# Two head transposes ahead of the fourth mLSTM numerator, and w_out's first tile begun with its pool rows in both banks

## The chip, the cores and the metric

The kernel runs on one core of one Trainium2 chip. The metric is the device time of one execution in microseconds, the median of several runs of the same program; lower is better. A core has a matrix engine (TensorE, PE in the profile; its weight loads are PEld), a vector engine (VectorE, DVE), a scalar engine (ScalarE, ACT), GpSimd (POOL) and SyncE (SP), which here issues most of the DMAs. Each works through its own queue in order; semaphores tie the queues together.

## What is computed

One inference step of a two-layer decoder for 512 prompt tokens and 8 sample tokens, all in float32. The first layer mixes by two parallel groups of channels, a causal pooling mixer and an mLSTM with four heads; both halves of the mix go through one output projection w_out (1024 x 1024). After it comes a mixture-of-experts layer with 32 experts, two per token; then an S5 state space layer with a GLU, a second mixture of experts and a last norm. Cut to the part that matters here:

```python
pool_out, pb = _pool_mixer(z[..., :o1], ...)            # 512 channels, four groups of 128
ml_out, c1, n1, m1 = _mlstm_mixer(...)                  # 512 channels, four heads of 128
mix = jnp.concatenate([pool_out, ml_out], axis=-1).astype(x.dtype) @ w['w_out_ab'][e]
x = x + mix.astype(x.dtype)
x = x + _hmoe(_rmsnorm(x, w['norm_ffn'][l]), ...)

# in _pool_mixer
y = jnp.einsum('btgc,gcd->btgd', d, pool_w.astype(jnp.float32)).reshape(uf.shape)
return y * pool_scale.astype(jnp.float32), ext[:, -POOL_BUF:]

# in _mlstm_chunk, for one chunk of 128 tokens
num = jnp.einsum('bhls,bhsd->bhld', s, v) + w_inter[..., None] * jnp.einsum('bhvk,bhlk->bhlv', c, q)
h = num / jnp.maximum(jnp.abs(den), jnp.exp(-m_row))[..., None]
# at the end of _mlstm_mixer
return hs * jax.nn.sigmoid(o_pre.astype(f32)), c1, n1, m1
```

## The kernel before, in words

The 512 prompt tokens are four chunks of 128. In the stage that the change touches, each chunk c gives a numerator product `num c` (TensorE, L797 and L799, with the denominators as a 129th column), which VectorE divides and stores as rows of heads, HM (L1754 to L1760, the body of one loop over c). TensorE then transposes the four heads of the chunk (`hT c`, in the helper `transposes`, L705), and VectorE multiplies them by the output gate into MIX (L1770, a second loop over c). MIX has eight blocks of 128 rows: blocks 0 to 3 are the pooling half, blocks 4 to 7 the heads. The pooling half comes from four products `pw g` (TensorE, L810), which ScalarE scales into MIX with three instructions each (L1353, L1355, L1357).

All of these results pass through a ring of four PSUM slots of two banks each. `jobs_of_kernel` lists the jobs in the order in which they take slots, with the engine that empties each; a job waits until the job four places ahead of it in that list has been emptied. So the order of the list, which has to be the order of TensorE's program, decides who waits for whose slot. Behind the last `hT`, the router stage gets the same four slots under fixed roles; ROLES names the jobs that were last in them.

The router stage computes `main(k)` for five tiles of tokens: MIX times w_out, 16 matmuls of 128x512 in four quarters of four (L863; each f32 matmul leaves two records in the trace, a transpose one). `main(0)` and the first quarter of `main(1)` come first, then the transposes of tile 0 (L880), which read X and so wait until VectorE has added tile 0's product to it (L1845, the function `mixed`). Router logits are L893, position matmuls L904 and L906, the gathering of the first experts' rows L934. The router of layer 1 uses the same code.

On VectorE, behind the four L1770, come a memset (L1849), three products of 128x4096 (at L1605, the line of the helper `tt`) for the state of the sample tokens, which need two broadcasts from DRAM (scratch_sdk, scratch_sdd), and then the router: `produce(0)` is `mixed(0)`. SyncE loads w_out when `z 19` is full, the broadcasts when `pw 3` is full, and four small S5 loads when `num 3` is full; GpSimd waits for the last of these with its S5 preparation (L2246). The experts' weights are asked for when the last tile has been mixed.

## Time and profile before

| what | us |
|---|---|
| median of 3 runs | 1092.79 |
| lowest run | 1092.39 |
| highest run | 2146.93 |
| the profiled execution, its own time | 1091.85 |
| its span | 1090.0 |
| TensorE busy in the span | 950.8 (87%) |
| VectorE busy | 416.2 (38%) |
| ScalarE busy | 182.8 (17%) |
| GpSimd busy | 375.8 (34%) |

The span runs from the first to the last instruction of one profiled execution; all times in rows are counted from its start. Busy times of TensorE are of pipelined matmuls with modelled ends, so they overlap. The stage in question lies between 190 and 305 us. A row that gives an idle time in square brackets names what ended it.

### The profile page before, as it was taken

How to read it: one execution, taken by the hardware profiler on the slowest of the kernel's cores; microseconds unless marked ns; L12 is line 12 of the kernel's file. 1: busy time of each engine (PE TensorE's matmuls, PEld its weight loads, DVE VectorE, ACT ScalarE, POOL GpSimd, SP SyncE). 2: the span in 40 equal slices, each digit the busy share in tenths (PEclk: the TensorE clock that was granted, in tenths of full speed). 3: DMA queues.
4: the chain of work that ended last, by engine and by line, in shares of the span. 5: the costliest groups of instructions: out<-in, count | busy, mean ns of one | idle time of the engine just before them, and what ended most of it. 6: DMA issues, size and time to landing. Idle time of an engine off the chain costs nothing.

```text
span 1090.0 us, 15860 instructions
## 1 busy us (share of the span) xinstructions
PE 950.8 (87%) x5716; PEld 577.3 (53%) x5716; DVE 416.2 (38%) x913; ACT 182.8 (17%) x353; POOL 375.8 (34%) x647
## 2 busy tenths in 40 slices
PE   3999989899897888787788499999989999787786
PEld 3788879545554444444444466444455555344342
DVE  5301155757752222232227762123465223221217
ACT  5311021222210000000016421102351000000003
POOL 1278900283256666656551730000020221101000
PEclk9999999899898999999999789999979999999998
DMA  7126860650669999999994744703047999999965
GB/s 257 39 78 218 295 259 3 254 183 20 247 265 395 423 420 416 421 402 409 393 364 145 110 107 182 328 29 146 19 182 275 421 421 424 423 424 425 425 270 214
DMA packets 45920, 292.39 MB, mean 268 GB/s; under 512 B 10609, under 2 KB 12017, under 8 KB 26391
## 3 DMA queue, kind: packets, MB, share of 16 engines
q1 hardware_dynamic: 35463, 270.29, 62.8%
q0 software_dynamic: 8640, 16.03, 3.9%
q10 hardware_dynamic: 1760, 5.31, 1.5%
q8 instruction: 35, 0.57, 0.2%
q14 instruction: 22, 0.18, 0.0%
HBM read 270.47 MB, written 36.80 MB: 282 GB/s over the span
## 4 chain that ended last, share of the span: by engine, by line
PE 56%; DMA 28%; DVE 6%; SPq 4%; issue 3%; POOL 2%; ACT 1%; POOLq 0%; DVEq 0%; ACTq 0%
DMA arena<-in_w_gu 18%; PE ps L739 13%; PE ps L863 10%; PE ps L1007 9%; PE ps L1204 5%; DMA arena<-in_w_down 4%; PE ps L997 3%; SPq L570 2%; DMA arena<-scratch_hd,idx_now 2%; PE ps L934 2%; PE ps L1162 2%; PE ps L1158 2%; DMA arena<-scratch_kp 2%; PE ps L893 2%; POOL arena L2345 2%
## 5 line engine op out<-in xcount | busy, mean ns | idle before, releaser
L1007 PE MATMUL ps<-arena 128*64 128x256 f32 x2048 | 239.1, 389 | 52.8 <-DMA arena<-in_w_gu 52.6
L1007 PEld LDWEIGHTS ps<-arena 128*64 128x64 f32 x2048 | 148.5, 140 | 143.9 <-DMA arena<-in_w_gu 44.7
L2246 POOL TENSOR_TENSOR arena<-arena 128x32 f32<-128x32 f32 (+5 forms) x232 | 117.5, 506 | 171.3 <-DMA arena<-in_s_d 73.8
L2345 POOL TENSOR_TENSOR arena<-arena 128x256 f32<-128x256 f32 (+3 forms) x192 | 132.7, 691 | 41.7 <-POOL arena L2345 41.4
L739 PE MATMUL ps<-arena 128*128 128x260 f32 x640 | 141.7, 383 | 0.0
L997 PE MATMUL ps<-arena 128*64 128x512 f32 x512 | 124.7, 631 | 13.8 <-DMA arena<-in_w_down 13.2
L739 PEld LDWEIGHTS ps<-arena 128*128 128x128 f32 x640 | 121.1, 190 | 18.7 <-issue 0.4
L863 PE MATMUL ps<-arena 128*128 128x512 f32 x256 | 118.7, 616 | 3.9 <-DVE arena L1770 3.7
L1989 DVE TENSOR_TENSOR arena<-arena,ps 128x128 f32<-128x128 f32 x64 | 18.3, 288 | 256.2 <-ACT arena L1454 256.1
L1454 ACT ACTIVATE arena<-ps 128x128 f32<-128x128 f32 x64 | 17.8, 278 | 467.8 <-PE ps L1007 467.8
L863 PEld LDWEIGHTS ps<-arena 128*128 128x128 f32 x256 | 48.6, 196 | 61.2 <-issue 60.1
L997 PEld LDWEIGHTS ps<-arena 128*64 128x64 f32 x512 | 37.6, 144 | 79.3 <-issue 68.2
L1605 DVE TENSOR_TENSOR arena<-arena 128x32 f32<-128x32 f32 (+17 forms) x101 | 62.4, 617 | 35.1 <-DMA arena<-scratch_rows 21.9
L2011 DVE TENSOR_TENSOR arena<-ps,arena 128x512 f32<-128x512 f32 x60 | 41.5, 691 | 77.2 <-PE ps L997 77.2
L428 POOL TENSOR_TENSOR arena<-arena 128x4 f32<-128x4 f32 (+1 forms) x8 | 1.6, 201 | 190.8 <-DVE arena L2218 164.4
L2388 POOL COPY idx_now<-idx_dest 128x1 int32 (+1 forms) x30 | 5.5, 184 | 167.0 <-DVE arena L2011 167.0
L1204 PE MATMUL ps<-arena 128*128 128x512 f32 x128 | 55.4, 593 | 0.4 <-DVE arena L2188 0.4
L958 PE MATMUL ps<-arena 128*128 128x128 f32 x256 | 38.7, 276 | 6.2 <-DMA arena<-scratch_hd,idx_now 6.1
L705 PE MATMUL ps<-arena 128*128 128x128 f32 (+6 forms) x218 | 26.9, 275 | 18.4 <-DVE arena L1244 15.2
L2379 POOL DMA_INDIRECT arena<-scratch_hd,idx_now x30 | 32.2, 1074 | 26.0 <-POOL idx_now L2376 26.0
L1927 DVE TENSOR_TENSOR arena<-ps,arena 128x512 f32<-128x512 f32 x64 | 41.0, 681 | 0.3
L1204 PEld LDWEIGHTS ps<-arena 128*128 128x128 f32 x128 | 24.2, 190 | 30.2 <-issue 29.4
(225 smaller groups left out, 975.1 us busy)
## 6 DMA issues: line engine op xcount, KB each, us to landing
arena<-in_w_gu SPq DMA_DIRECT2D x64, 2048.0 KB, 13.2
arena<-in_w_down SPq DMA_DIRECT2D x64, 1024.0 KB, 14.0
arena<-in_w_in SPq DMA_DIRECT2D x10, 1024.0 KB, 5.9
scratch_yd<-arena SPq DMA_DIRECT2D x2, 4160.0 KB, 18.6
arena<-scratch_yd SPq DMA_DIRECT2D x16, 512.0 KB, 7.3
arena<-in_w_out SPq DMA_DIRECT2D x1, 4096.0 KB, 12.2
scratch_hd<-arena ACTq DMA_DIRECT2D x8, 512.0 KB
arena<-in_w_glu SPq DMA_DIRECT2D x2, 2048.0 KB, 7.7
```

The lines of the kernel that those rows point to most:

```text
L739: mm = pe.matmul(o[:, b, 0:HALF], w[:, kc, (n % 2) * P:(n % 2 + 1) * P], HT[:, kc, b * HALF:(b + 1) * HALF], start=kc == 0, stop=kc == KC - 1)
L863: mm = pe.matmul(o[:, b, :], tokens_of(kc, i), w[:, kc, b * 512:(b + 1) * 512], start=kc == 0, stop=kc == KC - 1)
L958: mm = pe.transpose(ps[:, b, q * P:(q + 1) * P], XG[l][half][:, kc * P:(kc + 1) * P], ident)
L997: mm = pe.matmul(ps[CAP * s:CAP * s + CAP, 6 + b, :], AT[l][s][:, CAP * f:CAP * f + CAP], WD[l][i][b][:, 2 * s + f], start=f == 0, stop=f ...
L1007: mm = pe.matmul(ps[CAP * f:CAP * f + CAP, 2 + s, 0:256], XT[l][:, kc, CAP * s:CAP * s + CAP], WGU[l][i][s][:, kc, 256 * f:256 * f + 256], ...
L1204: mm = pe.matmul(o[0:n, b, :], YT[:, kc, i * P:i * P + n], WGL[0][:, kc, b * 512:(b + 1) * 512], start=kc == 0, stop=kc == KC - 1)
L1605: step(v.tensor_tensor(out, a, b, op))
L1927: v.tensor_tensor(XT[l][:, 4 * b:4 * b + 4], ps[:, b, :].rearrange("p (k t) -> p k t", k=4), spread(GK[:, l, 4 * b:4 * b + 4], P), ALU.mul ...
L2011: v.tensor_tensor(YE[l][half][:, 512 * b:512 * b + 512], ps[:, 6 + b, :], w, ALU.mult).then_inc(sem(f"y_ready_{l}"), 1)
L2246: step(g_.tensor_tensor(out, a, b, op))
L2345: g_.tensor_tensor(o, x, y, f).then_inc(sem("matrix_steps"), 1)
L2379: g_.indirect_dma_start(out=XG[l][half], out_offset=None, in_=hd, in_offset=bass.IndirectOffsetOnAxis(ap=now, axis=0), bounds_check=NT - 1 ...
```

## The change

Three things change, all in the order of work.

In the list of jobs and in TensorE's program, `hT 0` comes behind `pw 1`, `hT 1` behind `pw 2`, and `hT 2` behind `num 3`. `hT 3` is issued inside `main(0)`, behind its first quarter. ROLES names the new last four jobs of the ring.

The quarters of the first tile (k == 0, in both layers' routers) go through the banks in turn: contraction blocks 0 to 3 for bank 0, then for bank 1, then blocks 4 to 7 for bank 0, then for bank 1. Before, a bank was completed ahead of the other. The waits are spread over the quarters: the first for the pool rows, the third for `hT 3` to have been written out.

On VectorE, the first loop handles chunks 0 to 2, then heads 0 and 1 are written out, then chunk 3 is divided, then heads 2 and 3 are written out.

```diff
-    j += [(("pw", g), "act") for g in range(4)]
-    j += [(("num", 3), "dve")]
-    j += [(("hT", c), "dve") for c in range(TILES)]
+    j += [(("pw", 0), "act"), (("pw", 1), "act"), (("hT", 0), "dve"), (("pw", 2), "act"), (("hT", 1), "dve")]
+    j += [(("pw", 3), "act"), (("num", 3), "dve"), (("hT", 2), "dve"), (("hT", 3), "dve")]
...
-            jobs = [("hT", c) for c in range(TILES)] if l == 0 else [("gl", 0, i) for i in range(1, 5)]
+            jobs = [("pw", 3), ("num", 3), ("hT", 2), ("hT", 3)] if l == 0 else [("gl", 0, i) for i in range(1, 5)]
...
-            for g in range(4):
+
+            def pool_product(g):
                 pe.wait_ge(sem("pool_mixed"), g + 1)
                 ring.wait_free(pe, "pw", g)
...
-            numerator(3)
-            for c in range(TILES):
+
+            def heads(c):
                 ring.wait_emptied(pe, "num", c)
-                ring.wait_free(pe, "hT", c)
                 o = slot("hT", c)
                 transposes(("hT", c), [(o[:, 0, h * P:(h + 1) * P], HM[:, c, h]) for h in range(H)])
+            pool_product(0)
+            pool_product(1)
+            heads(0)
+            pool_product(2)
+            heads(1)
+            pool_product(3)
+            numerator(3)
+            heads(2)
             pe.wait_ge(sem("w_out_in"), 16)
-            for g in range(4):
-                ring.wait_emptied(pe, "pw", g)
-            ring.wait_emptied(pe, "hT", TILES - 1)
...
-                        b, k0 = q // 2, 4 * (q % 2)
+                        b, k0 = (q // 2, 4 * (q % 2)) if k else (q % 2, 4 * (q // 2))
...
-            router(0, MIX, lambda kc, i: MIX[:, kc, i * P:(i + 1) * P], WOUT, lambda q: None)
+            def mixed_ready(q):
+                if q == 0:
+                    for g in range(4):
+                        ring.wait_emptied(pe, "pw", g)
+                elif q == 1:
+                    heads(3)
+                elif q == 2:
+                    ring.wait_emptied(pe, "hT", TILES - 1)
+            router(0, MIX, lambda kc, i: MIX[:, kc, i * P:(i + 1) * P], WOUT, mixed_ready)
...
-            ring.wait_emptied(dve, "z", 19)
-            for c in range(TILES):
+
+            def heads_out(c):
                 take(dve, "hT", c)
...
+            for c in range(3):
+                heads_of(c)
+            ring.wait_emptied(dve, "z", 19)
+            heads_out(0)
+            heads_out(1)
+            heads_of(3)
+            heads_out(2)
+            heads_out(3)
```

TensorE, from the first pool product to the first w_out matmuls, with the semaphores that a row waits for (psum_emptied_by_dve and psum_emptied_by_act are the slots given back by VectorE and by ScalarE). Before, the end of the stage, from the last numerator's last product on (L705 are the head transposes, of which the first three groups read alike and one stands; L863 is w_out):

```order
L799 MATMUL ps<-arena 128x129
L705 MATMUL ps<-arena 128x128 [waits psum_emptied_by_act,psum_emptied_by_dve]
L705 MATMUL ps<-arena 128x128 x3
...
L705 MATMUL ps<-arena 128x128 [waits psum_emptied_by_dve]
L705 MATMUL ps<-arena 128x128 x3
L863 MATMUL ps<-arena 128x512 [waits psum_emptied_by_act,psum_emptied_by_dve,w_out_in]
L863 MATMUL ps<-arena 128x512 x15
```

The same place after the change, from the numerator's last product on (head transposes are now L704, w_out L867):

```order
L798 MATMUL ps<-arena 128x129
L704 MATMUL ps<-arena 128x128 [waits psum_emptied_by_act,psum_emptied_by_dve]
L704 MATMUL ps<-arena 128x128 x3
L867 MATMUL ps<-arena 128x512 [waits psum_emptied_by_act,w_out_in]
L867 MATMUL ps<-arena 128x512 x3
L704 MATMUL ps<-arena 128x128 [waits psum_emptied_by_dve]
L704 MATMUL ps<-arena 128x128 x3
L867 MATMUL ps<-arena 128x512 x4
L867 MATMUL ps<-arena 128x512 [waits psum_emptied_by_dve]
L867 MATMUL ps<-arena 128x512 x7
```

Two groups of head transposes have gone from here to places between the pool products, the fourth group stands behind the first quarter of w_out, and the wait for VectorE is in front of the third quarter. Ahead of the numerator, TensorE after the change, from the second pool product (L810) to the fourth:

```order
L810 MATMUL ps<-arena 128x260 [waits psum_emptied_by_act,pool_mixed]
L810 MATMUL ps<-arena 128x260
L704 MATMUL ps<-arena 128x128 [waits psum_emptied_by_dve]
L704 MATMUL ps<-arena 128x128 x3
L810 MATMUL ps<-arena 128x260 [waits psum_emptied_by_dve,pool_mixed]
L810 MATMUL ps<-arena 128x260
L704 MATMUL ps<-arena 128x128 [waits psum_emptied_by_act,psum_emptied_by_dve]
L704 MATMUL ps<-arena 128x128 x3
L810 MATMUL ps<-arena 128x260 [waits psum_emptied_by_act,pool_mixed]
L810 MATMUL ps<-arena 128x260
```

Before, the four pool products stood here one behind the other, and the numerator behind them. On VectorE, before, from the scaling of the fourth numerator (L1760) to the addition of tile 0 (L1845):

```order
L1760 TENSOR_SCALAR arena<-ps,arena 128x128 [waits dve_steps] x4
L1770 TENSOR_TENSOR arena<-ps,arena 128x4x32x4 [waits psum_full,psum_emptied_by_act,psum_emptied_by_dve]
L1770 TENSOR_TENSOR arena<-ps,arena 128x4x32x4 [waits psum_full,psum_emptied_by_dve] x3
L1849 MEMSET arena 128x1744 [waits psum_emptied_by_dve]
L1605 TENSOR_TENSOR arena<-arena 128x4096 [waits c0_in,kb_in,dve_steps]
L1605 TENSOR_TENSOR arena<-arena 128x4096 [waits dve_steps] x2
L1845 TENSOR_TENSOR arena<-arena,ps 128x1024 [waits dve_steps,routed]
```

After, from the scaling of the third numerator (now L1773) to the same addition (L1866):

```order
L1773 TENSOR_SCALAR arena<-ps,arena 128x128 [waits dve_steps] x4
L1783 TENSOR_TENSOR arena<-ps,arena 128x4x32x4 [waits psum_full,psum_emptied_by_act,psum_emptied_by_dve]
L1783 TENSOR_TENSOR arena<-ps,arena 128x4x32x4 [waits psum_full,psum_emptied_by_dve]
...
L1773 TENSOR_SCALAR arena<-ps,arena 128x128 [waits dve_steps] x4
L1783 TENSOR_TENSOR arena<-ps,arena 128x4x32x4 [waits psum_full,psum_emptied_by_dve] x2
L1870 MEMSET arena 128x1744 [waits psum_emptied_by_dve]
L1617 TENSOR_TENSOR arena<-arena 128x4096 [waits c0_in,kb_in,dve_steps]
L1617 TENSOR_TENSOR arena<-arena 128x4096 [waits dve_steps] x2
L1866 TENSOR_TENSOR arena<-arena,ps 128x1024 [waits dve_steps,routed]
```

Two of the four output products stand ahead of the fourth numerator's steps; the memset, the three long products and the addition follow as they did.

## Rows read from the trace of the kernel before

**Rows 1.** The page: span, and shares of the chain that ended last.
```profile
span 1090.0 us, 15860 instructions
...
PE 56%; DMA 28%; DVE 6%; SPq 4%; issue 3%; POOL 2%; ACT 1%; POOLq 0%; DVEq 0%; ACTq 0%
```
**Rows 2.** Chain of waits, 180 to 300 us: start us, us, what.
```profile
208.90 20.02 PE ps L863 x40
...
229.79 3.44 PE ps L863 x8
```
**Rows 3.** Timeline of TensorE, 182 to 330: start, us, engine, line, tiles, count, idle before.
```profile
195.75 2.79 PE L810 MATMUL ps<-arena 128*128 128x260 f32 x12
199.06 1.11 PE L810 MATMUL ps<-arena 128*128 128x260 f32 x4 [0.51 <-DVE arena L1760]
...
201.80 1.16 PE L705 MATMUL ps<-arena 128*128 128x128 f32 x8
...
208.90 20.02 PE L863 MATMUL ps<-arena 128*128 128x512 f32 x40 [3.73 <-DVE arena L1770]
228.75 1.04 PE L880 MATMUL ps<-arena 128*128 128x128 f32 x8
...
292.57 10.96 PE L934 MATMUL ps<-arena 128*128 128x512 f32 x20
```
**Rows 4.** Timeline of VectorE, 186 to 320 us.
```profile
195.05 1.51 DVE L1760 TENSOR_SCALAR arena<-ps,arena 128x128 f32<-128x128 f32 x4
...
197.41 1.51 DVE L1760 TENSOR_SCALAR arena<-ps,arena 128x128 f32<-128x128 f32 x4
202.07 0.16 DVE L1754 COPY arena<-ps 128x4 f32<-128x4 f32 x1 [3.15 <-PE ps L799]
...
204.42 4.22 DVE L1770 TENSOR_TENSOR arena<-ps,arena 128x512 f32<-128x512 f32 x4
209.07 1.51 DVE L1849 MEMSET arena<- 128x1744 f32 x1 [0.43 <-DMA arena<-scratch_sdk]
210.62 14.82 DVE L1605 TENSOR_TENSOR arena<-arena 128x4096 f32<-128x4096 f32 x3
225.59 1.22 DVE L1845 TENSOR_TENSOR arena<-arena,ps 128x1024 f32<-128x1024 f32 x1
```
**Rows 5.** Timeline of ScalarE: the last instructions of pool rows 1 and 3.
```profile
200.14 0.27 ACT L1357 ACTIVATE arena<-ps,arena 128x8 f32<-128x8 f32 x1
...
203.69 0.27 ACT L1357 ACTIVATE arena<-ps,arena 128x8 f32<-128x8 f32 x1
```
**Rows 6.** SyncE's queue: two issues; then DMA issues: KB, us to landing.
```profile
192.38 0.36 SPq L485 DMA_DIRECT2D arena<-in_w_out  x1
200.26 0.35 SPq L485 DMA_DIRECT2D arena<-scratch_sdk  x1
...
arena<-in_w_out SPq DMA_DIRECT2D x1, 4096.0 KB, 12.2
```
**Rows 7.** TensorE by stretches: window, us, busy (count), granted clock, DMA share, GB/s.
```profile
209.00:214.00 5.00, 5.00 (x6) 0.50 0.38 125
...
228.80:281.00 52.20, 52.20 (x227) 1.00 0.28 100
...
291.00:296.00 5.00, 4.38 (x9) 0.50 0.99 419
```
**Rows 8.** Timelines of GpSimd (120 to 330) and of VectorE (from 215.5).
```profile
128.13 1.27 POOL L2311 TENSOR_TENSOR arena<-arena 128x512 f32<-128x512 f32 x1
...
212.26 17.93 POOL L2246 TENSOR_TENSOR arena<-arena 128x512 f32<-128x512 f32 x6 [73.85 <-DMA arena<-in_s_d]
...
282.46 0.20 POOL L428 TENSOR_TENSOR arena<-arena 128x4 f32<-128x4 f32 x1 [25.90 <-DVE arena L1845]
...
215.08 10.36 DVE L1605 TENSOR_TENSOR arena<-arena 128x4096 f32<-128x4096 f32 x2
...
243.24 4.42 DVE L1605 TENSOR_TENSOR arena<-arena 128x4096 f32<-128x4096 f32 x1
```

More of the change, by code:

```diff
@@ L1750, in _, with heads_of @@
             dve.sem_inc(sem("mlstm_parts"), 1)
-            for c in range(TILES):
+            def heads_of(c):
                 take(dve, "num", c)
@@ L1764, in _ @@
                 give(dve, ins, "num", c)
-            ring.wait_emptied(dve, "z", 19)
-            for c in range(TILES):
+            def heads_out(c):
                 take(dve, "hT", c)
```

## The prediction

> **What bounds the kernel now.** The page first [rows 1]: a span of 1090.0 us, with 1091.85 us as that execution's own time (1.85 us lies around the span) and 1092.79 us as the median of the runs, so the profiled execution is 0.9 us under the median. The chain that ended last is 56% TensorE and 28% DMA. The change touches some 45 us of it. In the chain of waits cut to that piece [rows 2] the reader is to see this: from 208.90 it is TensorE's w_out matmuls L863, and it stays on TensorE behind the transposes L880; ahead of that it is VectorE's (the numerators' scaling L1760, then four L1770 products, [rows 4]). So on its face TensorE is what bounds the routing stage, and every us by which it starts earlier looks like a us won.
>
> TensorE's rows [rows 3] say how it comes to start at 208.90: it waits 3.73 us for the last L1770. VectorE's rows [rows 4] say what a chain of waits can't: behind L1770 VectorE has a memset, three 128x4096 products (the sample state update) and only then L1845, which adds tile 0's product to X. L1845 starts at 225.59, right as the third product ends (210.62 + 14.82 = 225.44), and has no wait in its row. TensorE's first group of transposes L880 needs L1845's result and starts at 228.75; L1845 ends at 226.81. So VectorE is only 1.9 us behind TensorE as a bound, and it is a full queue of work.
>
> **TensorE's part of the change.** Each f32 matmul leaves two records, a transpose one. A quarter of a w_out tile (four matmuls, 8 records) takes 3.44 us at full clock [rows 2]; one pool product 2.79/3 = 0.9 us, num 3 runs from 199.06 + 0.9 to 201.80 = 1.8 us, one head's transposes 1.16/2, about 0.5 us [rows 3]. In the new order: pool products 0 and 1 end at 197.5; head transposes 0 follow at once (their slot, num 1's, was freed by L1760 at 195.05 + 1.51 = 196.56 [rows 4]; head 0 was scaled before) and end at 198.0. Pool product 2 now needs num 2's slot: that is the wait that pool product 3 has today, released at 199.06. It ends at 199.9, head transposes 1 at 200.4. Pool product 3 needs pool product 1's slot, which ScalarE gives back at 200.14 + 0.27 = 200.41 [rows 5], and runs 200.55 to 201.4; num 3 to 203.2 (today 201.8, 1.4 us earlier); head transposes 2 to 203.7. ScalarE ends the four pool rows at 203.69 + 0.27 = 203.96 as today, since it is busy without a gap [rows 5]. Then w_out: issued at 192.38, 12.2 us to landing, so there at 204.6 [rows 6]. **TensorE starts w_out at 204.65 instead of 208.90, 4.25 us earlier**, and its waits on the way there are 1.0 and 0.9 us instead of 3.7.
>
> First quarter to 208.1, head transposes 3 (0.45 us) to 208.55, the other three quarters (3 x 3.44) to 218.9, the first quarter of tile 1 to 222.3. Today the same point is 228.75. That is 6.45 us: 4.25 us of start and 2.6 us of clock less 0.45 us of transposes moved in. The clock: after the 3.73 us wait the granted clock is 0.50 (1.2 GHz) from about 207 to 214, so 5.2 us of matmuls run at half rate and cost 2.6 us [rows 7].
>
> The two banks taken in turns cost nothing: the same 16 matmuls with the same 16 weights, in another order; router 1 gets the order too, and its one wait is still in its first quarter.
>
> **VectorE's part.** It has the same instructions, in another order. After head 2 (197.41 + 1.51 = 198.92) it writes out head 0 at once (to 200.0), head 1 when its transposes are there (200.65 to 201.7). Numerator 3 is full 1.4 us later than today, so its five small steps and four scalings start at about 203.5 instead of 202.07 and, taking 204.42 - 202.07 = 2.35 us, end at 205.8. Head 2 goes out by 206.9 (4.22/4 = 1.06 us each). VectorE is now 1.75 us ahead of today. But head 3's transposes stand behind the first quarter of w_out, which waits for its DMA: they end at 208.55, VectorE sees them at 208.8, and writes head 3 until 209.85. Today it ends at 208.64. **So VectorE leaves the stage 1.2 us later, not earlier.** Behind it, unchanged in order: 0.43 us to the memset, 1.51 us, then 14.82 us of products [rows 4], and L1845 from 226.8 to 228.0. The products also wait for two broadcasts that SyncE issues from 200.26 on [rows 6] and that are there at 210.62, when the first product starts without a wait [rows 4]. Their issue waits for pool product 3 and moves to about 201.7; they stand in the queue behind w_out until 204.6 anyway, so I leave them there by 210.6, 1.2 us ahead of the products' new start of 211.8. If they moved by their whole 1.4 us, it would be 212.0, 0.2 us more.
>
> **Where the gain goes.** Transposes L880 of tile 0 start at max(222.3, 228.0 + 0.14) = 228.1 (0.14 us lies today between L1760's end at 198.92 and the pool product that it releases, 199.06), against 228.75: of 6.45 us, 0.6 us is left. And TensorE now idles 222.3 to 228.1, 5.8 us, longer than the 3.73 us after which its clock fell. So it runs at 1.2 GHz afterwards. In today's case the low stretch behind such a wait is 5.2 us, worth 2.6 us; nothing at all is the other end. I take 2.2 us, near the row: the array has been busy up to the wait, where today it was sparse for 6 us. The 2.6 us that this stretch costs today are not won back, they move behind the wait, and there no VectorE lag covers any of them. Sum: -0.6 + 2.2 = **+1.6 us**.
>
> From 228.8 on TensorE runs without a gap up to 281 (busy in all 52.2 us of the window [rows 7]), VectorE keeping up with it; the late 128x4096 pair there moves along. The weight DMAs of the experts are issued after L1845 of the last tile, and the expert loop takes turns between gu_done and those loads, so it moves as a whole. GpSimd, behind its S5 preparation, waits 25.9 us for its next work [rows 8], so its loads, issued up to 1.4 us later behind num 3, cost nothing; if that cover were gone they would cost that 1.4 us. I therefore carry +1.6 us to the end: 1091.85 + 1.6 = 1093.5 against its own time, and **1094.4 us** against the median of 1092.79.
>
> **A rule against the order.** Today the first 128x4096 product starts before GpSimd's 128x512 ones and takes 4.4 us (14.82 - 10.36, [rows 4, 8]); the later two, beside them, take 5.17 us each against 4.42 us for one later on, and GpSimd's take 17.93/6 = 3.0 us against 1.27 us for one alone [rows 8]. If VectorE, 1.2 us later, meets GpSimd at work from its first product, that product costs 5.17 too, 0.75 us more. GpSimd starts at 212.26, or later since its loads are issued later, so I count none, and put the 0.75 us into the range. The Trainium skill (SBUF — State Buffer, "SBUF: two separate sides") says that VectorE with two SBUF inputs and GpSimd take a shared port pair as a lock for a whole instruction, the loser blocked. By that VectorE could lose a whole 1.27 us instruction each time; the rows show 0.75 us on each product, and they decide.
>
> **Rivals.**
> (a) TensorE's gain comes through (chance 0.10). VectorE's products would have to be off the path: 1092.8 - 6.45 = 1086.3. For it: the chain names TensorE. Against it: L1845's row, which starts 0.15 us behind a product and not behind TensorE. It decides if L1845 starts below 222.
> (b) The clock doesn't fall in the new wait (0.10): -0.6 us, 1092.2. Against it: today the wait of 3.73 us, with sparse work ahead of it, is followed by a clock of 0.50 [rows 3, 7].
> (c) On the slower side (0.13): the second stretch at half clock, 285 to 296 [rows 7], gets longer. TensorE's L934 (20 records in 10.96 us from 292.57 [rows 3]) runs its first matmuls at 0.50: 20 records of 0.86 us would be 17 us, so some 4 to 5 of them ran slow and about 16 at the full rate. Moved by 1.6 us against whatever brings the clock back, half of these 16 full-rate records (0.43 us each) may fall into the low stretch: 3.4 us, so 1.6 + 3.4 = 5.0, 1097.8. It decides if the granted clock is still 0.50 two us after L934 began.
> (d) The order does nothing at all, +-0.5 us (0.02): against it speak 4.25 us of TensorE start.
>
> **How the numbers follow.** The forecast, VectorE late and the clock low, has 0.65: its own range is 1092.7 (only 0.5 us lost to the clock) to 1095.6 (2.6 us, and 0.75 us of port). Range 1090.5 to 1098.0: it takes in b, c and d, b also when counted from the profiled execution's own time (1091.85 - 0.6 = 1091.2, less the 0.4 us between the two closest runs), and leaves a out. Faster by over 2% would need 21.9 us, which no case holds; slower by over 2% neither; 2% is about what a measurement of this kernel can tell from no change, so nearly all of the chance is within it.
>
> **What would show it.** Right: L863 of w_out starts at about 204.7; the last L1783 (today's L1770) ends at about 209.9; the first 128x1024 add starts at about 226.8 with no wait for TensorE; TensorE's first transposes of tile 0 have a wait of about 5.8 us put down to that add; a granted clock of 0.50 right after it. Wrong: that add earlier than 225.6, or a w_out DMA that lands after 206 and holds the transposes of head 3 further, or a time outside the range through the expert loop.

## The result, and the profile after

| what | before | after |
|---|---|---|
| median of 20 runs each | 1094.05 | 1095.49 |
| ratio over the paired rounds, with 95% interval | | 1.0025 [1.0014, 1.0037] |
| the profiled execution, its own time | 1091.85 | 1094.67 |
| its span | 1090.0 | 1092.8 |

In this comparison the change made the kernel a little slower. The ratio is worth 2.7 us (1.5 to 4.0), the two medians lie 1.4 us apart, and the two profiled executions 2.8 us. All of it is inside the 2% that count as no change, and 1095.49 is inside the range. The forecast was 1094.4 us, that is +1.6 us. Ratios are formed over paired rounds, so they can differ from the ratio of two medians; they leave out single executions, of the kernel before as of variants, that took 1609 to 4251 us.

The page's head and the chain's shares by engine, to be read against [rows 1]: VectorE's share of the chain has grown from 6% to 8%, and its line L1617 (before: L1605) now stands in the list.

```profile
span 1092.8 us, 15860 instructions
PE 54%; DMA 26%; DVE 8%; SPq 4%; issue 4%; POOL 3%; ACT 1%; POOLq 0%; DVEq 0%; ACTq 0%
```

TensorE's timeline after (start, duration, group, and in brackets the idle time and what ended it). In the new numbering L704 are the head transposes, L867 w_out, L884 the transposes of a tile, L938 the gathering of the first experts' rows. It answers [rows 3].

```profile
199.14 1.11 PE L810 MATMUL ps<-arena 128*128 128x260 f32 x4 [0.95 <-DVE arena L1773]
...
204.63 3.70 PE L867 MATMUL ps<-arena 128*128 128x512 f32 x8 [0.66 <-DMA arena<-in_w_out]
208.17 0.60 PE L704 MATMUL ps<-arena 128*128 128x128 f32 x4
...
228.23 1.94 PE L884 MATMUL ps<-arena 128*128 128x128 f32 x8 [5.73 <-DVE arena L1866]
229.97 4.11 PE L867 MATMUL ps<-arena 128*128 128x512 f32 x8
...
246.00 1.04 PE L884 MATMUL ps<-arena 128*128 128x128 f32 x8
246.87 3.60 PE L867 MATMUL ps<-arena 128*128 128x512 f32 x8
...
294.37 11.64 PE L938 MATMUL ps<-arena 128*128 128x512 f32 x20
```

The reader is to see three things. The wait for the last head has gone (3.73 us in [rows 3]), w_out starts 4.27 us earlier, and its product runs through from 204.63 to about 222.5. Then there is a new wait of 5.73 us, put down to L1866, the add that was L1845. And behind it the same two groups take 1.94 and 4.11 us that take 1.04 and 3.60 us 18 us later: they run at a lower clock.

VectorE's timeline after, which answers [rows 4] (L1783 writes heads out, L1870 is the memset, L1617 the 128x4096 products, L1866 the add):

```profile
208.88 1.04 DVE L1783 TENSOR_TENSOR arena<-ps,arena 128x512 f32<-128x512 f32 x1 [1.83 <-PE ps L704]
210.35 1.51 DVE L1870 MEMSET arena<- 128x1744 f32 x1 [0.43 <-DMA arena<-scratch_sdk]
211.90 14.82 DVE L1617 TENSOR_TENSOR arena<-arena 128x4096 f32<-128x4096 f32 x3
226.87 1.22 DVE L1866 TENSOR_TENSOR arena<-arena,ps 128x1024 f32<-128x1024 f32 x1
```

VectorE waits 1.83 us for head 3's transposes, which stand behind the first quarter of w_out, and leaves the stage at 209.92. From there everything is shifted by 1.28 us against [rows 4], through to the add.

The chain of waits cut to this piece shows who carries the time now (before, [rows 2], it was TensorE from 208.90 on):

```profile
201.84 0.35 SPq L484
...
202.24 9.29 DMA arena<-scratch_sdd
...
211.56 0.31 DVE arena L1870
...
211.90 4.44 DVE arena L1617
...
226.87 1.23 DVE arena L1866
...
228.23 1.94 PE ps L884 x8
```

Between 211.5 and 228.1 it is VectorE alone. Ahead of that the profile names not the head but a broadcast: scratch_sdd, issued at 202.24, right behind scratch_sdk (201.84), and landed at 211.53. The memset behind head 3 ends at 211.86, only 0.33 us behind this landing: this matters below.

TensorE's busy time and granted clock by stretch after (stretch, its length, PE busy, records, clock, DMA share, GB/s), which answers [rows 7]:

```profile
222.00:226.00 4.00, 0.51 (x2) 1.00 0.00 0
...
228.00:231.00 3.00, 2.77 (x10) 0.50 0.97 399
231.00:282.00 51.00, 50.90 (x218) 1.00 0.25 96
...
286.00:294.00 8.00, 7.35 (x35) 0.50 0.92 321
294.00:298.00 4.00, 4.00 (x8) 0.50 1.00 424
```

The stretch at 0.50 (1.2 GHz) that lay behind the wait for the heads (209 to 214 in [rows 7]) now lies behind the wait for the add. The second one, from 286 on, is there as before, and lasts until about 299 instead of 296.

The 2.8 us of the two spans, split at points that both kernels have: 0.1 up to the first pool product; -0.6 from there to tile 0's transposes; +1.4 to tile 1's add (the clock); 0.0 to the last add; +1.6 to the first expert matmul; +0.4 in the expert loop; -0.1 in the rest.

### The profile page after: what moved, and what is told of

Same layout as the page of the kernel before. It is cut to its first block, busy times and chain, and to the rows that moved or that the text cites. A ratio compares the mean times of both kernels' runs of the same rounds, so it can differ in the third digit from the quotient of the medians.

```text
span 1092.8 us, 15860 instructions
## 1 busy us (share of the span) xinstructions
PE 947.1 (87%) x5716; PEld 577.9 (53%) x5716; DVE 415.9 (38%) x913; ACT 182.9 (17%) x353; POOL 375.1 (34%) x647
## 4 chain that ended last, share of the span: by engine, by line
PE 54%; DMA 26%; DVE 8%; SPq 4%; issue 4%; POOL 3%; ACT 1%; POOLq 0%; DVEq 0%; ACTq 0%
DMA arena<-in_w_gu 17%; PE ps L738 13%; PE ps L867 9%; PE ps L1011 9%; PE ps L1216 5%; DMA arena<-in_w_down 4%; PE ps L1001 3%; DVE arena L1617 3%; POOL arena L2366 2%; SPq L569 2%; DMA arena<-scratch_hd,idx_now 2%; PE ps L938 2%; PE ps L1174 2%; PE ps L1170 2%; PE ps L897 2%
## 5 line engine op out<-in xcount | busy, mean ns | idle before, releaser
L1001 PE MATMUL ps<-arena 128*64 128x512 f32 x512 | 119.2, 607 | 13.4 <-DMA arena<-in_w_down 12.9
L867 PE MATMUL ps<-arena 128*128 128x512 f32 x256 | 116.8, 607 | 0.8 <-DMA arena<-in_w_out 0.7
L867 PEld LDWEIGHTS ps<-arena 128*128 128x128 f32 x256 | 47.9, 194 | 56.3 <-issue 54.3
L1617 DVE TENSOR_TENSOR arena<-arena 128x32 f32<-128x32 f32 (+17 forms) x101 | 62.0, 613 | 34.9 <-DMA arena<-scratch_rows 22.0
L704 PE MATMUL ps<-arena 128*128 128x128 f32 (+6 forms) x218 | 26.8, 272 | 18.0 <-DVE arena L1256 15.9
```

The lines of the kernel that those rows point to most:

```text
L867: mm = pe.matmul(o[:, b, :], tokens_of(kc, i), w[:, kc, b * 512:(b + 1) * 512], start=kc == 0, stop=kc == KC - 1)
L1001: mm = pe.matmul(ps[CAP * s:CAP * s + CAP, 6 + b, :], AT[l][s][:, CAP * f:CAP * f + CAP], WD[l][i][b][:, 2 * s + f], start=f == 0, stop=f ...
L1617: step(v.tensor_tensor(out, a, b, op))
```

## The experiments

Theory A is the prediction's: VectorE's queue (head 3, memset, three products, add) decides when tile 0 can be transposed, so TensorE's 4.3 us are spent in a wait, and that wait costs clock. Against it stand that the difference comes from somewhere else (the order of banks, the broadcasts' later issue, the last router stage, the expert loop), or that it is chance.

The profiled executions are compared by the time from the start of the first pool product (L810), in us. The last stage is from the last tile's add to the first expert matmul. The column "expert loop" is what follows it, up to the first matmul of the GLU (L1204 before), so it holds the first experts and the state space layer.

| kernel | tile 0's transposes | tile 1's add | last add | first expert matmul | last stage | expert loop | span |
|---|---|---|---|---|---|---|---|
| before | 33.00 | 46.24 | 85.41 | 111.58 | 26.17 | 365.69 | 1090.0 |
| r1_before_mix_early | 33.33 | 46.57 | 85.74 | 111.97 | 26.23 | 369.67 | 1095.4 |
| r2_banks_only | 31.91 | 45.14 | 84.32 | 112.11 | 27.79 | 369.85 | 1096.6 |
| after | 32.39 | 46.99 | 86.17 | 113.97 | 27.80 | 366.11 | 1092.8 |
| r1_after_again | 32.76 | 47.86 | 87.03 | 114.85 | 27.82 | 366.84 | 1096.0 |
| r2_heads3_first | 32.28 | 47.22 | 86.40 | 114.16 | 27.76 | 370.31 | 1097.2 |
| r3_after_third | 32.82 | 49.01 | 88.19 | 114.36 | 26.17 | 366.73 | 1093.6 |
| r1_after_fill | 32.41 | 45.71 | 84.89 | 111.48 | 26.59 | 366.86 | 1093.5 |
| r3_fill_again | 32.41 | 45.70 | 84.88 | 111.34 | 26.46 | 366.56 | 1091.6 |
| r1_after_mix_early | 27.39 | 40.65 | 79.82 | 107.57 | 27.75 | 367.38 | 1086.8 |
| r2_mix_first | 26.56 | 39.79 | 80.15 | 107.87 | 27.72 | 365.94 | 1087.4 |
| r2_mix_fill2 | 27.29 | 40.55 | 79.72 | 105.52 | 25.80 | 369.79 | 1088.5 |
| r3_mix_fill3 | 27.16 | 40.42 | 79.60 | 103.11 | 23.51 | 368.26 | 1081.7 |
| r4_before_fill3 | 33.46 | 46.70 | 85.87 | 109.39 | 23.52 | 365.73 | 1086.2 |

That piece takes 365.7 to 370.3 us, in kernels of either order and with no visible relation to the edits; nearly all of the spread is in the experts themselves (256.0 to 261.3 us from their first gate and up matmul, L1007 before, to their last). So a total moves by up to 4.6 us for a reason outside the change, and differences of 1 to 2 us are read from the columns ahead of it.

### The changed kernel once more, twice

> The changed kernel unaltered, as the yardstick of this group. Both theories: +2.7 us against before (ratio 1.0025), the first 128x1024 add at about 226.9, a wait of TensorE of 5.7 us for it.

Measured: 1097.13 us (12 runs) against 1094.05, ratio 1.0008 [0.9992, 1.0023]. The medians lie 3.1 us apart, the ratio is worth 0.9 us: this comparison alone doesn't tell the two kernels apart.

> The changed kernel once more, as the yardstick of this group. From the first pool product to tile 1's add: 47.0 to 47.9 us, as in its two profiles so far (before: 46.2). Total +1 to +3 us against before.

Measured: 1096.53 us (12 runs) against 1093.03, ratio 1.0024 [1.0006, 1.0042].

With the first comparison there are three ratios, 1.0025, 1.0008 and 1.0024: the change costs somewhere between nothing and 4 us. The profiles say more. The wait for the add is 6.17 us in the second execution and 6.07 us in the third, and the low clock behind it lasts differently long each time. Second and third execution, TensorE's timeline, first two groups behind the wait:

```profile
229.51 1.94 PE L884 MATMUL ps<-arena 128*128 128x128 f32 x8 [6.17 <-DVE arena L1866]
231.25 4.60 PE L867 MATMUL ps<-arena 128*128 128x512 f32 x8
```

```profile
228.38 1.94 PE L884 MATMUL ps<-arena 128*128 128x128 f32 x8 [6.07 <-DVE arena L1866]
230.11 5.69 PE L867 MATMUL ps<-arena 128*128 128x512 f32 x8
```

Against 1.04 and 3.60 us at full clock, the wait costs 0.90 + 0.51 = 1.4 us in the first profile, 1.9 in the second and 3.0 in the third.

These sizes can be read from the granted clock. In all three it had fallen to 0.50 (1.2 GHz) during the wait, between 226.4 and 227.6, and it rose again at 231.0, 233.3 and 234.3. From the end of the wait (228.23, 229.51, 228.38) that is 2.8, 3.8 and 5.9 us of work at half rate, and half of each is the 1.4, 1.9 and 3.0 us lost. The third execution:

```profile
228.00:234.00 6.00, 5.62 (x13) 0.50 1.07 314
```

The old order pays in the same way behind the wait for the heads. Its 40 records of w_out take 20.02 us in the kernel before, 20.33 in r1_before_mix_early, 18.92 in r2_banks_only and 20.47 in r4_before_fill3, against 17.33 us with the clock at 1.00 throughout (r2_heads3_first): 1.6 to 3.1 us.

### Tile 0's add moved ahead of the third product

```diff
             tt(kb4, kb4, spread(vs.rearrange("p h n -> p n h"), P), ALU.mult)
+            mixed(0)
             tt(CS, CS, KB, ALU.add)
...
-                produce(0)
+                if l:
+                    produce(0)
```

> The changed kernel, with the add of tile 0 (mixed(0)) put between the second and the third 128x4096 product on VectorE instead of behind the third. Theory A (TensorE's 4.2 us are real and are lost only because VectorE's products stand ahead of the add): the add at about 221.6, TensorE's wait for it 0.7 us instead of 5.7, no half clock there, transposes of tile 0 at about 223.0 instead of 228.2; tile 1's add at 236.9 instead of 242.8; about 5.9 us less than the changed kernel if all of it reaches the end, so 3 us under before. Theory B (the new order costs in itself, by its banks or its waits): transposes move as said, but the total stays at before's time or above, within 1 us of the changed kernel.

Measured: 1088.61 us (7 runs), ratio 0.9943 [0.9921, 0.9964], 6.2 us faster than before. VectorE's and TensorE's timelines:

```profile
212.07 9.62 DVE L1617 TENSOR_TENSOR arena<-arena 128x4096 f32<-128x4096 f32 x2
221.73 1.22 DVE L1866 TENSOR_TENSOR arena<-arena,ps 128x1024 f32<-128x1024 f32 x1
222.98 5.26 DVE L1617 TENSOR_TENSOR arena<-arena 128x4096 f32<-128x4096 f32 x1
```

```profile
223.10 1.06 PE L884 MATMUL ps<-arena 128*128 128x128 f32 x8 [0.51 <-DVE arena L1866]
224.00 3.60 PE L867 MATMUL ps<-arena 128*128 128x512 f32 x8
```

The wait is 0.51 us instead of 5.73, its two groups run at the full rate, and tile 0's transposes come 5.0 us earlier. Taking a single product (5.2 us) out of VectorE's way turned a small loss into a gain of half a per cent. That is theory A. Expected were 5.9 us under the changed kernel; at tile 1's add it is 6.3 to 8.4 us (three profiles of it), by the medians of this round 8.5.

### The same move in the kernel before

> The kernel before, with the same move of mixed(0) between the second and third product. In it w_out's tile 0 ends only at 225.3, when VectorE has nothing else to wait for: the add would stand at 225.5 and the third product behind it. Theory A: no gain, 0 to +1 us against before (the third product ends 4 us later, which the sample products at 258 don't feel). Theory B, that VectorE's order alone is what can be won: 3 us or more under before.

Measured: 1094.5 us (12 runs), ratio 0.9993 [0.9977, 1.0009]. VectorE now waits for TensorE at the add, and tile 0's transposes come no earlier (33.33 against 33.00 in the table):

```profile
211.33 9.62 DVE L1605 TENSOR_TENSOR arena<-arena 128x4096 f32<-128x4096 f32 x2
226.53 1.22 DVE L1845 TENSOR_TENSOR arena<-arena,ps 128x1024 f32<-128x1024 f32 x1 [5.58 <-PE ps L863]
```

Before the change both engines bound this point within 1.9 us of each other, so the earlier add alone is worth nothing, the earlier w_out alone nothing or a small loss, and the two together 6 us.

### The add moved one product further

```diff
+            mixed(0)
             tt(kb4, kb4, spread(vs.rearrange("p h n -> p n h"), P), ALU.mult)
-            mixed(0)
             tt(CS, CS, KB, ALU.add)
```

> The changed kernel, with mixed(0) between the first and the second product instead of the second and third. The add has to wait 2.6 us for TensorE (tile 0 ends at 218.9) and comes at 219.1; TensorE's wait for it goes from 0.5 us to nothing, the third product ends 2 us later. Theory A: 0 to 1 us less than with the other place, or up to 2 us more if the later products hold up the add of the third tile (253.2 to 256 then).

Measured: 1089.78 us (8 runs), ratio 0.9969 [0.9952, 0.9986]. TensorE now has no wait ahead of tile 0's transposes, and is 0.8 us earlier there than with the add behind two products. It doesn't last. VectorE's timeline: the add waits 2.85 us in the middle of the queue, so the third product ends 2.1 us later than with the add behind two products (230.38 against 228.24). The broadcast of scratch_sdq goes out only then, at 230.46 instead of 228.33, and the product that needs it finds it missing:

```profile
219.22 1.22 DVE L1866 TENSOR_TENSOR arena<-arena,ps 128x1024 f32<-128x1024 f32 x1 [2.85 <-PE ps L867]
...
239.81 4.44 DVE L1617 TENSOR_TENSOR arena<-arena 128x4096 f32<-128x4096 f32 x1 [2.96 <-DMA arena<-scratch_sdq]
```

That product starts at 239.81, where with the add behind two products it starts at 237.61. By the last add it is 0.3 us behind that kernel (80.15 against 79.82). The two totals, measured in different rounds, are 3.4 and 6.2 us under before, and their intervals overlap: they don't rank the two places. The gain ends where TensorE's own product ends.

### TensorE kept busy through the wait

Six needless matmuls of 128x512 go, in the changed kernel, into a free slot between w_out's first quarter of tile 1 and tile 0's transposes. Nobody reads them.

```diff
+                    if l == 0 and k == 0:
+                        first_use(SMALL_ROLE)
+                        for kc in range(6):
+                            pe.matmul(role(l, SMALL_ROLE)[:, 0, :], tokens_of(kc, 0), w[:, kc, 0:512], start=True, stop=True)
```

> The changed kernel, with six needless 128x512 matmuls (12 records, 5.2 us at full clock) into a free PSUM slot, issued while TensorE waits 5.7 us for the add of tile 0. Their result is never read. Theory A with the clock term: granted clock stays 1.00 at 228 to 231 instead of 0.50, tile 1's add comes 1.5 us earlier than in the changed kernel (241.3), total 1.5 us less than it. If the clock term is nothing: the same total as the changed kernel, within 0.5 us.

Measured: 1095.18 us (12 runs), ratio 0.9996 [0.9975, 1.0018]. TensorE's timeline (here L884 are the needless ones, L888 the transposes) and its clock:

```profile
223.12 5.31 PE L884 MATMUL ps<-arena 128*128 128x512 f32 x12
228.91 1.09 PE L888 MATMUL ps<-arena 128*128 128x128 f32 x8 [0.48 <-DVE arena L1870]
229.84 3.60 PE L867 MATMUL ps<-arena 128*128 128x512 f32 x8
```

```profile
226.00:230.00 4.00, 3.52 (x15) 1.00 0.42 131
230.00:234.00 4.00, 4.00 (x17) 1.00 1.06 315
```

> The changed kernel with the six needless matmuls in TensorE's wait for the add of tile 0, once more, since its first comparison was too wide to tell 1.5 us. Clock theory: 45.7 us from the first pool product to tile 1's add, 1.3 to 2.2 us under the changed kernel's, and a total 1.5 us under it. Rival: the total is the changed kernel's within 0.5 us.

Measured: 1096.62 us (12 runs), ratio 1.0032 [1.0017, 1.0046].

The two profiles agree: with the transposes at the same place (32.41 against 32.39), tile 1's add comes at 45.7, where the changed kernel has 47.0 to 49.0. So the clock's cost at this wait is real, 1.3 to 3.3 us, and it is the clock's, not the transposes'. The totals don't show it: by the medians the kernel is 1.95 us under the changed kernel of the same round the first time and 0.09 us over it the second, by the ratios 1.3 us under and 0.9 us over. Each ratio is good to 1.6 to 2.4 us, so neither 1.5 us nor nothing can be excluded, and that the saving reaches the end is not shown. The one profiled execution of the second comparison has it still at the first expert matmul (111.34 against 114.36).

### Head 3's transposes ahead of w_out

```diff
             heads(2)
+            heads(3)
             pe.wait_ge(sem("w_out_in"), 16)
...
-                elif q == 1:
-                    heads(3)
```

> The changed kernel, with the fourth group of head transposes issued ahead of the wait for w_out instead of behind w_out's first quarter. Theory A1 (VectorE is late only because these transposes stand behind the first quarter; and the broadcast for its products, which landed at 211.56 in the changed kernel, is the next bound): the last head is written out by 208.2 instead of 209.9, but the first 128x4096 product starts at about 211.65 instead of 211.90, TensorE's w_out at 206.7 instead of 204.65; total 0.3 us less than the changed kernel, not to be told from it. Theory A2 (the broadcast doesn't bind): the first product starts at 210.2, the add of tile 0 at 225.1, and the total is 1.7 us less than the changed kernel.

Measured: 1097.52 us (10 runs), ratio 1.0027 [1.0012, 1.0043]. The head is now out at 208.06 and VectorE free 1.9 us earlier, and yet its products start at 211.73 against 211.90. VectorE's timeline:

```profile
208.49 1.51 DVE L1869 MEMSET arena<- 128x1744 f32 x1 [0.43 <-DVE arena L1782]
211.73 14.82 DVE L1616 TENSOR_TENSOR arena<-arena 128x4096 f32<-128x4096 f32 x3 [1.72 <-issue]
```

Behind the head, 0.2 us away, stands the broadcast of the chain above. The bracket says "issue", that is, the profile doesn't name what VectorE waited for. The row of that DMA in the same execution does: it is issued at 202.17 and takes 9.5 us to landing, so it is there at 211.67, 0.06 us ahead of the product.

```profile
arena<-scratch_sdd SPq DMA_DIRECT2D x1, 16.0 KB, 9.5
```

In r1_after_again the product waits for it too, with head 3 in its place (the row of DMA issues has 10.0 us for it there, so 213.14):

```profile
203.14 9.57 DMA arena<-scratch_sdd
212.71 0.47 issue
213.18 4.44 DVE arena L1617
```

TensorE's w_out starts 1.8 us later here (206.44), which costs nothing, since TensorE still waits 4.29 us for the add. So head 3's place inside w_out was not alone in costing the time: head 3 and the broadcast each hold the first product to about the same moment, and taking one away gains 0.2 us. I would expect the same end of any order that issues the broadcasts behind `pw 3` with two heads' transposes ahead of it; no run here tries another.

### The order of banks alone

```diff
-                        b, k0 = q // 2, 4 * (q % 2)
+                        b, k0 = (q // 2, 4 * (q % 2)) if k else (q % 2, 4 * (q // 2))
```

> The kernel before, with nothing changed but the order of the quarters of the first tile of each router (banks in turn). Theory A: no difference, 0 +- 0.5 us, and tile 0 takes the same time on TensorE, 13.8 us at full clock. Theory B (taking banks in turn costs): tile 0 takes longer than four quarters of 3.44 us, and the total rises by twice that.

Measured: 1094.61 us (10 runs), ratio 0.9993 [0.9976, 1.0011]. No cost and no gain. That its profile has tile 0's transposes 1.1 us earlier than the kernel before (31.91 against 33.00) is the clock, which rose at 212.9 here and at 214.1 there, behind a wait that ended at 209.89 here and at 208.90 there. The profile has a use of its own: the last stage takes 27.79 us here, with TensorE's order at the end of the mLSTM as before.

### Wide matmuls in the small waits of the router

The changed kernel's last stage is at half clock from 286 to 299. The next two kernels put needless 128x512 matmuls, again read by nobody, into its short waits; both routers have them. r2_mix_fill2, on top of the moved add:

```diff
+                def idle_work(n):
+                    for _ in range(n):
+                        pe.matmul(main_slot(l, 1)[:, 1, :], ident, X[:, 0, 0:512], start=True, stop=True)
...
+                idle_work(1 + l)
                 transpose(4)
                 position(3)
+                idle_work(1)
                 logits(4)
                 for k in range(4):
                     pe.wait_ge(sem("ranked"), 5 * l + k + 1)
                     list_part(0, k)
+                idle_work(1)
                 position(4)
```

> The version with mixed(0) between the second and third product, plus one or two needless 128x512 matmuls (never read) in three short waits of TensorE at the end of each router stage (before the last transposes, before the last logits, before the last position). Theory C (half of what the changed kernel lost came from the second stretch at half clock, 285 to 299): granted clock stays at 1.00 over 278 to 292 in at least one of the two layers, and the time from the last tile's add to the first expert matmul falls from 27.8 to about 25 us, in layer 1 likewise; total 2 to 5 us under that version. If the short waits aren't what lowers the clock there: the clock falls as before and the total rises by 0 to 2 us, for the added matmuls.

Measured: 1085.97 us (6 runs), ratio 0.9921 [0.9906, 0.9936]. The last stage takes 25.80 us instead of 27.75; the clock is held up to about 285 and then still is at 0.50 until about 291.

r3_mix_fill3 has one in the loop, and two behind it instead of one:

```diff
                     list_part(0, k)
-                idle_work(1)
+                    if k == 1:
+                        idle_work(1)
+                idle_work(2)
```

> The version with mixed(0) between the products and needless matmuls in the waits at the end of the router stages, with two more of these ahead of the last position matmul. If the clock falls at 285 only for want of wide matmuls: it stays at 1.00 to 290, and the last add to the first expert matmul takes 24.5 us instead of 25.8; total 0 to 2 us under r2_mix_fill2's 1086. If not: 26.5 us or more, since the added matmuls then stand in the way, and the total 0 to 2 us above it.

Measured: 1081.81 us (6 runs), ratio 0.9882 [0.9856, 0.9909]: 12.9 us faster than before, the best of all. It is more than was expected, both in the stage (24.5 us) and in the total (0 to 2 us under r2_mix_fill2). TensorE's stretches in the last stage and the gathering matmuls (L947 here, 11.64 us in the changed kernel):

```profile
286.00:290.00 4.00, 4.00 (x14) 1.00 1.00 409
290.00:294.00 4.00, 4.00 (x10) 1.00 0.99 419
```

```profile
286.88 9.22 PE L947 MATMUL ps<-arena 128*128 128x512 f32 x20
```

The last stage takes 23.51 us, and the corresponding part of layer 1 is 3.7 us shorter than in the kernel before (159.94 to 156.29 us from the GLU's start to the second experts).

> The kernel before, with only the needless matmuls (never read) of r3_mix_fill3 in the waits at the end of both router stages. If the two gains of that version are separate and add up: the clock stays at 1.00 to the end of the stage, last add to first expert matmul 23.5 us instead of 26.2, the same in layer 1, and 4 to 7 us under before (ratio 0.994 to 0.996), with mixed(0)'s move worth the other 6 us. If most of the 12 us is the needless matmuls' own: 10 us or more. If they need the other move to help: within 2 us of before.

Measured: the same needless matmuls in the kernel before, 1086.36 us (6 runs) against 1094.21, ratio 0.9929 [0.991, 0.9947]; last stage 23.52 us. These 7.8 us are a little more than the 4 to 7 expected; 2.7 us are in the last stage and 3.7 in layer 1. The two gains are separate: 0.9943 x 0.9929 = 0.9873, beside 0.9882 measured together.

## Why the prediction was right, step by step

**TensorE's start, right.** w_out at 204.63 (predicted 204.65), put down to its DMA. The head transposes of chunk 3 end at 208.61 (208.55).

**VectorE leaves later, right.** 209.92 against 209.85, first product 211.90 against 211.8, add 226.87 against 226.8 with no wait in its row. The moved add shows that this is the bound, with 5.0 us behind it. But the reason given for it, head 3 behind w_out's first quarter, is only one of two: by r2_heads3_first the broadcast alone would have held the first product to 211.7.

**The broadcasts, wrong, but in the bounds.** The step "I leave them there by 210.6" failed. Their issues moved by 1.58 us (scratch_sdk from 200.26 in [rows 6] to 201.84), and the landing moved with them: scratch_sdd came at 211.53, where before it came 9.7 us behind an issue at 200.66, at 210.36, though w_out was on the queue until 204.6 in both. That these two landings lie only 1.2 us apart is within the scatter of executions: scratch_sdd takes 9.7 to 10.0 us to landing in three profiles of the old order, 9.3 to 10.0 in eight of the new one. The rows of the two kernels' DMA issues (KB, us to landing), before and after:

```profile
arena<-scratch_sdd SPq DMA_DIRECT2D x1, 16.0 KB, 9.7
```

```profile
arena<-scratch_sdd SPq DMA_DIRECT2D x1, 16.0 KB, 9.3
```

The other case that the prediction named (212.0, "0.2 us more") is the nearer one: 0.33 us of the memset were still to run when it landed in the changed kernel's profile, but in r1_after_again VectorE waited 0.48 us and in r3_after_third 0.38. I had taken the queue ahead for a cover without a row that showed it.

**Where the gain goes, right.** The wait is 5.73 us (5.8), tile 0's transposes start at 228.23 (228.1), 0.52 us earlier than before; 0.6 was forecast.

**The clock, right in kind and about in size.** 2.2 us were taken. The three executions lost 1.4, 1.9 and 3.0 us to it, and r2_heads3_first's 1.7: 2.0 on average. The upper bound of 2.6, today's stretch, was too low: the clock rose 2.8 to 5.9 us behind the end of the wait, which one row can't show. The Trainium skill (TensorE: Matmul & The Clock Gate, "Part 1: The HAM clock gate") says that the number of slow matmuls at a kernel's start differs from run to run of the same kernel. Behind this wait, inside a kernel, the profiles show the same, with 4.11, 4.60 and 5.69 us for the same eight records.

**The port, no cost.** The first product takes 4.44 us as before (chain); it had begun 1.3 us ahead of GpSimd, which starts at 213.22. The 0.75 us of the range weren't needed. One reading beside them was off: the 3.0 us of GpSimd are a mean of two kinds. Three of its six 128x512 instructions run beside the products and take 4.0, 5.1 and 5.3 us (3.7, 5.1 and 5.3 before), three behind them take 1.1 to 1.3 us. Each long one ends 0.9 to 1.1 us behind the end of a product, and the product that began in the meantime takes 0.75 us longer. That looks like whole instructions taking turns, as the rule in the prediction has it, and not against it; GpSimd's times are rough, and no run was made for this.

**Rival (a)** was the state of things only once VectorE was taken out of the way: 1088.6 us with the moved add, not 1086.3, since VectorE's first two products still hold the add to 221.73.

**Rival (b)** fell: the clock went to 0.50. **Rival (d)** fell by the rows, w_out being 4.27 us earlier and the add 1.28 us later; r1_after_again's total alone would not exclude it.

**Rival (c) came in part, its cause is not shown.** Its mark, a clock of 0.50 two us after the gathering matmuls began, decides nothing: [rows 7] have it in the kernel before (from 292.57 on, 0.50 up to 296). What it forecast, a longer stretch, did come: the gathering matmuls take 11.64 us instead of 10.96, and the whole stage is 1.6 us longer, not 3.4. But r2_banks_only has these 27.8 us in the old order, and r3_after_third 26.2 us in the new one. The stage takes one of two lengths, and it goes with the stretch at half clock, here in before, after, r3_after_third and r2_banks_only:

```profile
286.00:296.00 10.00, 9.38 (x32) 0.50 0.95 375
```

```profile
286.00:299.00 13.00, 12.35 (x42) 0.50 0.96 363
```

```profile
289.00:299.00 10.00, 9.42 (x29) 0.50 0.96 366
```

```profile
285.00:298.00 13.00, 12.33 (x42) 0.50 0.99 385
```

Some 3 us more at half rate are 1.5 us of work lost, about the 1.6 us. One of the three profiles of the old order without needless matmuls in the router has the long stretch, and five of the eight of the new one (the short ones are r3_after_third, r1_after_fill and r3_fill_again): too few to say that the change brings it.

**The sum.** +1.6 us were forecast. Up to tile 1's add the four profiles of the changed order (with the add behind the third product) stand at 47.8 on average, the three of the old at 46.0: +1.8, the part that was worked out; with r4_before_fill3, the same up to there, the old ones stand at 46.2, and it is +1.6. Up to the first expert matmul it is 114.3 against 111.9, +2.4, and 2.7 (1.5 to 4.0) by the ratio. The 0.6 us more than at tile 1's add are the last stage's; that they come from the change stays open. How close the totals came is in part luck. The forecast stood on a median of 3 runs, 1092.79; on the 20-run median of 1094.05 it would have been 1095.7, beside 1095.49. And the 1.4 us between the medians here are the smallest of three comparisons: in the two repeats it is 3.1 and 3.5 us.

## What to carry to other kernels

Where a chain names one engine, look for the first instruction that needs both it and another engine's result, and see how far the other engine is behind; here 1.9 us out of 6.5 was all that could be gained, whatever TensorE did. An in-order queue is changed where its late consumer's result is produced: the add that released TensorE stood behind a product that nobody waited for yet, and swapping these two, together with the earlier start, brought 6 us. A wait on TensorE can cost its own length and the clock behind it (1.4 to 3.0 us here). Where it can't be removed, wide matmuls in it can pay: in the router's short waits they brought 7.8 us, while at the one long wait the saving didn't show in the total. And where two waits end within 0.5 us of each other, as head 3 and the broadcast do, taking away one shows only the other.

## What the hardware showed that I had not expected

From 286 to 298 in the changed kernel, TensorE stands as busy (7.35 of 8 us, then 4.00 of 4), with matmuls of 36 and 32 columns and then the 128x512 ones of L938, and the granted clock is 0.50 throughout. A TensorE that the profile calls busy may still be at half rate, and here it stayed there through a run of narrow matmuls. With 4 needless wide matmuls put between them and one ahead of the tile's transposes, the clock is 1.00 in every stretch from 270 to 302 and the stage is 4.3 us shorter than in the changed kernel, although TensorE has more to do. In the old kernel they shorten it by 2.7 us, and in all they took 7.8 us off that kernel (ratio 0.9929). Whether it is the filled waits or the width of the added matmuls that holds the clock, no run separates.

The wait at tile 0 of some 6 us left the clock at 0.50 for 2.8 us behind it in one execution and for 5.9 in another, with the same program and nearly the same wait; and the piece with the experts took 365.7 to 370.3 us.
